# Gate columns of two convolution feed-forward layers: both activation parts in one 512-column product, added after PSUM

## The chip, the cores and the metric

One Trainium2 chip, one of its cores. The metric is the device time of one execution of the whole program in microseconds, as the median of several runs; a profile of one further execution gives the durations. The engines are called TensorE (PE in the profile; its weight loads are PEld), VectorE (DVE), ScalarE (ACT), GpSimd (POOL) and SyncE (SP), which here only starts transfers.

## The reference

Two transformer blocks over 256 tokens of width 1024, in float32. The change is in one function, which the second block calls once in each of its two layers:

```python
def conv_ffn(h, w_up, conv_w, conv_b, w_down):
    S = h.shape[1]
    u = h @ w_up                                        # 256 x 1024 @ 1024 x 5632
    up = jnp.pad(u, ((0, 0), (CONV_WIDTH_2 - 1, 0), (0, 0)))
    c = conv_b
    for i in range(CONV_WIDTH_2):                       # three taps along the tokens
        c = c + up[:, i:i + S] * conv_w[i]
    gate, val = c[..., :D_FF_2], c[..., D_FF_2:]        # 2816 each
    return (jax.nn.silu(gate) * val) @ w_down
```

The first block has a feed-forward layer without the convolution (`_swiglu`, "ffn0" in the kernel), which the change leaves as it is. The two with the convolution are "ffn1" and "ffn2". ffn2 is the last thing before the final norm.

## The kernel before

**Split products.** Nearly all products are done in three float32r matmuls. A weight tile W is split into w_hi, W rounded to float32r, and w_lo = W - w_hi; the activations likewise into a_hi and a_lo (inputs of a stage) or b_hi and b_lo (inputs of the second product of a stage). Each product is w_hi·a_hi + w_hi·a_lo + w_lo·a_hi, summed in PSUM (`three`, L468). A matmul loads a 128x128 weight block and streams 256 columns (the tokens) through it.

**Weights.** They come in slots of 8 blocks of 128x128 (512 KB) into a ring of six raw buffers (`w_raw`). For each slot ScalarE makes w_hi (L1187), and then VectorE makes w_lo (L1756), or for some slots GpSimd (L2602; `lo_on_pool` says which). w_hi and w_lo have rings of three, so the split of slot n may start only when TensorE is done with slot n-3. A slot gives TensorE 24 matmuls.

**A convolution feed-forward layer** (`ffn` in each engine's program). The 2816 hidden channels are 22 tiles of 128, f = 0 to 21. Per tile f there are three slots, in TensorE's order: the gate columns (g = 0), the value columns (g = 1), each 8 blocks over the 1024 inputs into one accumulator (PSUM banks 0 and 1 in turn), and the down product of an earlier tile (usually f-1), whose 8 outputs are kept in banks 4 to 7. In the two convolution layers GpSimd makes w_lo of the gate slots of f = 3 to 21, VectorE all others.

All engines' programs are written out in a fixed order, and an engine does its instructions in that order. For a tile f in the middle of the layer VectorE does:

1. g = 0: wait for the gate product; multiply the accumulator by the norm's factor into an SBUF tile (L2338, the eviction; it frees the accumulator); wait for ScalarE's first convolution tap (L1631); add the second tap (L2345) and the third (L2347);
2. g = 1: the same four for the value product;
3. wait for ScalarE's silu (L1640); multiply gate by value (L2359);
4. w_lo of the next tile's value slot (L1756), b_lo of the activation (L2371, after ScalarE's b_hi, L1650), w_lo of this tile's down slot (L1756); then the next tile.

ScalarE, for the same tile: the first tap of g = 0 (L1631), w_hi of the next tile's gate slot (L1187), the first tap of g = 1, silu, w_hi of the next value slot, b_hi, w_hi of the down slot. GpSimd waits for w_hi of the next tile's gate slot and makes its w_lo.

What ties them: TensorE can start a slot when its w_hi and w_lo are there, and an accumulator's next product when the eviction of the one before in that bank is done.

```python
x = FS[:, 2 * (f % 3) + g, :]
t = (name, 2 * f + g)
v.tensor_tensor(x, acc(t)[:, 0:T], R[:], ALU.mult).then_inc(
    *inc("ffn_scaled", ("fs", tag, f, g), ("acc", t)))
```

Of the kernel before, what the change touches and what calls it, by code (L numbers as in the profile page):

```python
# [17 lines left out]
P = 128  # L18
T = 256
D = 1024  # L20
KD = D // P
# [173 lines left out]
class Signals:  # L195
# [16 lines left out]
    def inc(self, label, *events, by=1):  # L212
        sem = self.sem(label)
        self.counts[label] += by
        for e in events:
            assert e not in self.events, e
            self.events[e] = (label, self.counts[label])
        return sem, by
# [48 lines left out]
def build(nc, io, known):  # L267
    with ExitStack() as ctx:
# [3 lines left out]
        def sb(name, shape, dt=F32):  # L272
            return ctx.enter_context(nc.sbuf_tensor(name, shape, dt))
# [3 lines left out]
                "p (a b) -> p a b", a=KD) for i in range(2))  # L277
        WHI = sb("w_hi", [P, SPLIT_SLOTS, 1024], F32R)
        WLO = sb("w_lo", [P, SPLIT_SLOTS, 1024], F32R)
        AH, AL = sb("a_hi", [P, KD, T], F32R), sb("a_lo", [P, KD, T], F32R)  # L280
        BH, BL = sb("b_hi", [P, KD, T], F32R), sb("b_lo", [P, KD, T], F32R)
        RAW = sb("w_raw", [P, RAW_SLOTS, 1024])
        H = sb("h", [P, KD, T])
# [43 lines left out]
        def acc(key):  # L327

            return bank[ACC_BANK[key]]
# [119 lines left out]
        def _(pe):  # L449
# [14 lines left out]
            def three(out, w, x, start, stop, weights_move=False, check=False):  # L464

                for n, (wi, xi) in enumerate(((0, 0), (0, 1), (1, 0))):
                    l, r = (x[xi], w[wi]) if weights_move else (w[wi], x[xi])
                    ins = mm(out, l, r, start=start and n == 0, stop=stop and n == 2, skip_group_check=check)  # L468
                return ins

            def blocks(s, b, n=1):
                c = slice(b * P, (b + n) * P)
                return WHI[:, ring(s), c], WLO[:, ring(s), c]

            def pair(x, k, cols=slice(0, T)):
                return x[0][:, k, cols], x[1][:, k, cols]
# [430 lines left out]
            def ffn(name, tag):  # L907

                s = FIRST[name]
                for f in range(NF + 1):  # L910
                    if f < NF:
                        for g in range(2):
                            out = acc_take((name, 2 * f + g))[:, 0:T]
                            slot_ready(s)
                            for k in range(KD):
                                if f == 0 and g == 0:
                                    pe.wait_ge(*at(("a_lo", tag, k)))
                                ins = three(out, blocks(s, k), pair(A, k), k == 0, k == KD - 1)
                            ins.then_inc(*inc("product_done", ("slot", s), (name, f, g)))
                            s += 1  # L920
                            if f == 0 and g == 0:
                                if tag in SUMMED:
                                    whole_mean_square(tag)
                                else:
                                    mean_square(tag, KD - 2)
                                    mean_square(tag, KD - 1)
                    for d in down_after(f):
                        slot_ready(s)
                        pe.wait_ge(*at(("act_lo", tag, d)))
                        for m in range(KD):  # L930
                            ins = three(bank[4 + m // 2][:, m % 2 * T:m % 2 * T + T], blocks(s, m),
                                        pair(B, d % 3), d == 0 and m % 2 == 0, f == NF, check=True)
                            if f == NF and m % 2 and m < KD - 1:
                                ins.then_inc(*inc("product_done", (name, "bank", m // 2)))
                        ins.then_inc(*inc("product_done", ("slot", s), (name, "down", d),
                                                      *([(name, "bank", 3)] if f == NF else [])))
                        s += 1
# [808 lines left out]
        def _(dve):  # L1746
# [14 lines left out]
            def step(ins, *events, label="vector_step"):  # L1761

                ins.then_inc(*inc(label, *events))
                dve.wait_ge(*last(label))
# [559 lines left out]
            def ffn(name, tag, tag_next, g_next, conv=None):  # L2324
                s = FIRST[name]
                ahead(s + 1)
                dve.wait_ge(*at(("r", tag)))
                for f in range(NF + 1):
                    if f < NF:
                        for g in range(2):  # L2330
                            ahead(s)
                            s += 1
                            dve.wait_ge(*at((name, f, g)))
                            if f >= 3 and conv is None:
                                dve.wait_ge(*at(("fa", tag, f - 3)))
                            x = FS[:, 2 * (f % 3) + g, :]
                            t = (name, 2 * f + g)
                            v.tensor_tensor(x, acc(t)[:, 0:T], R[:], ALU.mult).then_inc(  # L2338
                                *inc("ffn_scaled", ("fs", tag, f, g), ("acc", t)))
                            if f == 0 and g == 1:  # L2340
                                ahead(FIRST[name] + 2)
                            if conv is not None:
                                c = FC[:, 2 * (f % 2) + g, :]
                                dve.wait_ge(*at(("fc", tag, f, g)))
                                step(v.scalar_tensor_tensor(c[:, 1:T], x[:, 0:T - 1], par(f"cw{conv}", 44 + g * NF + f),  # L2345
                                                            c[:, 1:T], ALU.mult, ALU.add), label="ffn_conv")
                                v.scalar_tensor_tensor(c[:, 2:T], x[:, 0:T - 2], par(f"cw{conv}", g * NF + f),  # L2347
                                                       c[:, 2:T], ALU.mult, ALU.add).then_inc(
                                    *inc("ffn_conv", ("fcv", tag, f, g)))
                        dve.wait_ge(*at(("silu", tag, f)))  # L2350
                        if conv is not None:
                            dve.wait_ge(*at(("fcv", tag, f, 1)))
                        else:
                            dve.wait_ge(*at(("fs", tag, f, 1)))
                        if f >= 2:
                            dve.wait_ge(*at(("act_lo", tag, f - 2)))
                        src = (FS[:, 2 * (f % 3), :], FS[:, 2 * (f % 3) + 1, :]) if conv is None else \
                            (FC[:, 2 * (f % 2), :], FC[:, 2 * (f % 2) + 1, :])
                        v.tensor_tensor(FA[:, f % 2, :], src[0], src[1], ALU.mult).then_inc(  # L2359
                            *inc("ffn_act", ("fa", tag, f)))  # L2360
                    for n, _ in enumerate(down_after(f)):
                        if n == 0 or f == NF:
                            ahead(s + n)
                    s += len(down_after(f))
                    if name == "ffn0" and f == 9:
                        final_weights()
                    if name == "ffn0" and f == 11:
                        rope_args()
                    if f < NF:
                        dve.wait_ge(*at(("act_hi", tag, f)))  # L2370
                        v.tensor_tensor(BL[:, f % 3, :], FA[:, f % 2, :], BH[:, f % 3, :].bitcast(F32),  # L2371
                                        ALU.subtract).then_inc(*inc("ffn_act_lo", ("act_lo", tag, f)))
                    if f == NF - 1:
                        ahead(s - 1)
                for m in range(KD):
                    if m % 2 == 0:
                        dve.wait_ge(*at((name, "bank", m // 2)))
                    step(v.tensor_tensor(H[:, m, :], H[:, m, :], bank[4 + m // 2][:, m % 2 * T:m % 2 * T + T], ALU.add),
                         ("h", tag_next, m), label="h_made")
                    if g_next and m:  # L2380
                        lo_gained(tag_next, m - 1, A, H[:, m - 1, :], g_next)
                    if tag_next in NEXT_V and m in (4, 6):
                        ahead(SLOT[NEXT_V[tag_next], (m - 4) // 2])
                if g_next:
                    lo_gained(tag_next, KD - 1, A, H[:, KD - 1, :], g_next)
                if tag_next in NEXT_V:
                    ahead(SLOT[NEXT_V[tag_next], 2])
# [427 lines left out]
```

## Time and profile before

| | |
|---|---|
| time of three runs, median (lowest to highest) | 1211.64 us (1208.93 to 1212.19) |
| the profiled execution, its own time | 1210.1 us |
| its span | 1208.3 us |
| granted TensorE clock, mean | 0.995 of full speed |
| busy: TensorE / VectorE / ScalarE / GpSimd | 98% / 68% / 54% / 18% of the span |
| chain that ended last: TensorE / VectorE / ScalarE | 84% / 9% / 4% |

The page of the profile gives busy time by engine and by group of instructions; the lists in order of time ("timeline") give the start of each instruction, its duration and, in brackets, how long its engine sat idle before it and what ended that. The duration of a matmul is from its start to its modelled end, and matmuls overlap: the pace is read from the distance of their starts.

### The profile page before, as it was taken

To read this page: it belongs to the slowest core of one execution; us is meant where nothing else is said; L and a number is where in the kernel's file an instruction comes from. 1 tells how busy PE (TensorE), PEld (TensorE's weight loads), DVE (VectorE), ACT (ScalarE), POOL (GpSimd) and SP (SyncE) were. 2 spreads that over 40 slices of the span, in tenths; PEclk is the share of its full clock that TensorE was granted. 3 is DMA by queue.
4 is the path that set the end of the run, shared out by engine and by line. 5 is a ranking of instruction groups with operands and counts; after the bars stand their busy time and mean duration, and the time that the engine had idled before them with its cause. 6 is when DMAs were issued, how large, how long until landed. Compare 5 with 4: busy or idle time off the path is not lost.

```text
span 1208.3 us, 24091 instructions
## 1 busy us (share of the span) xinstructions
PE 1180.0 (98%) x9816; PEld 1111.9 (92%) x9816; DVE 819.6 (68%) x1472; ACT 656.3 (54%) x1128; POOL 214.6 (18%) x124
## 2 busy tenths in 40 slices
PE   9999999999999999999999999999999999999997
PEld 8888789999999999898898999999898878999997
DVE  6997856745544544678775776767655667777776
ACT  4347446645544444564566555555655566555554
POOL 2120000201122222021100223231121100322220
PEclk9999999999999999999999999999999989999999
DMA  8433334525656565543344566665433433665651
GB/s 342 139 108 115 112 124 141 168 94 181 199 179 188 178 188 177 162 137 100 114 140 145 170 187 180 188 179 171 160 124 121 140 123 109 187 189 179 189 178 36
DMA packets 51661, 188.60 MB, mean 156 GB/s; under 512 B 5728, under 2 KB 5856, under 8 KB 51040
## 3 DMA queue, kind: packets, MB, share of 16 engines
q1 hardware_dynamic: 51552, 187.07, 49.1%
q8 instruction: 78, 1.28, 0.4%
q14 instruction: 31, 0.25, 0.1%
HBM read 186.00 MB, written 1.05 MB: 155 GB/s over the span
## 4 chain that ended last, share of the span: by engine, by line
PE 84%; DVE 9%; ACT 4%; issue 2%; DMA 0%; POOL 0%; DVEq 0%; ACTq 0%
PE banks L468 65%; PE banks L498 7%; DVE w_lo L1756 2%; ACT w_hi L1187 2%; PE banks L541 1%; PE banks L972 1%; PE banks L526 1%; PE banks L986 1%; PE banks L589 1%; PE banks L952 1%; ACT arena L1631 1%; PE banks L889 1%; PE banks L866 1%; DVE arena L2345 1%; DVE arena L2347 0%
## 5 line engine op out<-in xcount | busy, mean ns | idle before, releaser
L1187 ACT ACTIVATE w_hi<-w_raw 128x1024 fp32r<-128x1024 f32 x313 | 328.9, 1052 | 179.4 <-PE banks L468 179.2
L468 PE MATMUL banks<-a_hi,w_hi 128*128 128x256 f32 x1432 | 410.7, 287 | 2.1 <-DVE w_lo L1756 1.1
L468 PE MATMUL banks<-a_lo,w_hi 128*128 128x256 f32 x1432 | 405.1, 283 | 0.0
L468 PE MATMUL banks<-a_hi,w_lo 128*128 128x256 f32 x1432 | 405.0, 283 | 0.0
L2602 POOL TENSOR_TENSOR w_lo<-w_raw,w_hi 128x1024 fp32r<-128x1024 f32 x80 | 194.8, 2435 | 844.5 <-ACT w_hi L1187 844.5
L1756 DVE TENSOR_TENSOR w_lo<-w_raw,w_hi 128x1024 fp32r<-128x1024 f32 x233 | 290.3, 1247 | 65.8 <-ACT w_hi L1187 64.6
L468 PEld LDWEIGHTS banks<-a_hi,w_hi 128*128 128x128 f32 x1432 | 274.5, 192 | 5.2 <-issue 3.5
L468 PEld LDWEIGHTS banks<-a_lo,w_hi 128*128 128x128 f32 x1432 | 274.6, 192 | 0.4
L468 PEld LDWEIGHTS banks<-a_hi,w_lo 128*128 128x128 f32 x1432 | 274.6, 192 | 0.0
L468 PE MATMUL banks<-b_hi,w_hi 128*128 128x256 f32 x880 | 253.6, 288 | 7.6 <-DVE h L2201 2.4
L468 PE MATMUL banks<-b_lo,w_hi 128*128 128x256 f32 x880 | 248.9, 283 | 0.0
L468 PE MATMUL banks<-b_hi,w_lo 128*128 128x256 f32 x880 | 248.8, 283 | 0.0
L468 PEld LDWEIGHTS banks<-b_hi,w_hi 128*128 128x128 f32 x880 | 168.6, 192 | 12.5 <-issue 4.1
L468 PEld LDWEIGHTS banks<-b_lo,w_hi 128*128 128x128 f32 x880 | 168.7, 192 | 0.3
L468 PEld LDWEIGHTS banks<-b_hi,w_lo 128*128 128x128 f32 x880 | 168.6, 192 | 0.0
L1631 ACT ACTIVATE arena<-arena,pars 128x256 f32<-128x256 f32 x88 | 53.0, 602 | 129.1 <-DVE arena L2338 129.1
L2338 DVE TENSOR_TENSOR arena<-banks,rstd 128x256 f32<-128x256 f32 x132 | 55.7, 423 | 86.9 <-PE banks L468 86.7
L2345 DVE SCALAR_TENSOR_TENSOR arena<-arena,pars 128x255 f32<-128x255 f32 x88 | 58.4, 664 | 57.7 <-ACT arena L1631 57.7
L498 PE MATMUL banks<-early,w_raw 128*128 128x256 f32 x368 | 82.0, 381 | 0.4 <-DVE early L1796 0.4
L498 PEld LDWEIGHTS banks<-early,w_raw 128*128 128x128 f32 x368 | 69.2, 190 | 10.6 <-DMA w_raw<-in_weights 0.6
L1650 ACT ACTIVATE b_hi<-arena 128x256 fp32r<-128x256 f32 x66 | 27.5, 417 | 39.1 <-DVE arena L2359 39.1
L1213 ACT ACTIVATE a_hi<-h,pars 128x256 fp32r<-128x256 f32 x64 | 32.2, 503 | 24.8 <-DVE h L2201 16.9
(396 smaller groups left out, 1311.3 us busy)
## 6 DMA issues: line engine op xcount, KB each, us to landing
w_raw<-in_weights SPq DMA_DIRECT2D x342, 512.0 KB, 3.6
arena<-in_mem SPq DMA_DIRECT2D x2, 1024.0 KB, 9.7
h<-in_x SPq DMA_DIRECT2D x1, 1024.0 KB, 5.3
early<-in_mem SPq DMA_DIRECT2D x1, 1024.0 KB, 15.5
out_h<-h SPq DMA_DIRECT2D x4, 256.0 KB, 2.6
cons<-in_cons SPq DMA_DIRECT2D x1, 546.0 KB, 7.8
arena<-in_late SPq DMA_DIRECT2D x1, 448.0 KB, 4.2
pars<-in_pars SPq DMA_DIRECT2D x1, 290.5 KB, 2.8
```

What stands on the lines that cost most here:

```text
L468: ins = mm(out, l, r, start=start and n == 0, stop=stop and n == 2, skip_group_check=check)
L498: ins = mm(out, raw(s, b % 8), x[:, k, :], start=n == 0, stop=n == K - 1)
L526: ins = mm(out, x[:, k, cols], raw(s, b * w % 8, w), start=k == 0, stop=k == K - 1)
L541: ins = mm(bank[2][:, 0:T] if out is None else out, ONES_D[:] if by is None else by, squares, start=m == 0, stop=m == KD - 1)
L1187: do(WHI[:, ring(n), :], RAW[:, n % RAW_SLOTS, :], ACT.Copy).then_inc(*inc("w_hi_made", ("w_hi", n)))
L1213: do(x[0][:, m, :], src, ACT.Copy, scale=par(g, m)).then_inc(*inc("input_hi", ("a_hi", tag, m)))
L1631: do(FC[:, 2 * (f % 2) + g, :], FS[:, 2 * (f % 3) + g, :], ACT.Identity, scale=par(f"cw{conv}", 88 + g * NF + f), bias=par(f"cb{conv}", g ...
L1650: do(BH[:, f % 3, :], FA[:, f % 2, :], ACT.Copy).then_inc(*inc("ffn_act_hi", ("act_hi", tag, f)))
L1756: v.tensor_tensor(WLO[:, ring(n), :], RAW[:, n % RAW_SLOTS, :], WHI[:, ring(n), :].bitcast(F32), ALU.subtract).then_inc(*inc("w_lo_made", ...
L2338: v.tensor_tensor(x, acc(t)[:, 0:T], R[:], ALU.mult).then_inc(*inc("ffn_scaled", ("fs", tag, f, g), ("acc", t)))
L2345: step(v.scalar_tensor_tensor(c[:, 1:T], x[:, 0:T - 1], par(f"cw{conv}", 44 + g * NF + f), c[:, 1:T], ALU.mult, ALU.add), label="ffn_conv")
L2602: g.tensor_tensor(WLO[:, ring(n), :], RAW[:, n % RAW_SLOTS, :], WHI[:, ring(n), :].bitcast(F32), ALU.subtract).then_inc(*inc("w_lo_pool", ...
```

## The change

- The split activations a_hi and a_lo of a stage are now two halves of one buffer, `a_parts`, so that for each of the 8 input blocks they lie side by side.
- In ffn1 and ffn2, for the gate slots alone (g = 0), w_hi is loaded once per block and streams a_hi and a_lo as one matmul of 512 columns: w_hi·a_hi goes to the left half of the accumulator's bank, w_hi·a_lo to the right half. w_lo·a_hi (256 columns) is added into the left half. 16 matmuls per gate slot instead of 24, with as many columns.
- VectorE then adds the two halves from PSUM with a tensor_reduce over pairs that lie 256 elements apart (the accumulator is free after it), and after a wait for its own result multiplies the SBUF tile by the norm's factor in place. The value slots keep their one multiplication.

```diff
-        AH, AL = sb("a_hi", [P, KD, T], F32R), sb("a_lo", [P, KD, T], F32R)
+        A_PARTS = sb("a_parts", [P, KD, 2, T], F32R)
+        AH, AL = (A_PARTS[:, :, i, :] for i in range(2))
...
-                                ins = three(out, blocks(s, k), pair(A, k), k == 0, k == KD - 1)
+                                if name != "ffn0" and g == 0:
+                                    w = blocks(s, k)
+                                    mm(acc((name, 2 * f + g)), w[0], A_PARTS[:, k, :, :].rearrange("p a b -> p (a b)"),
+                                       start=k == 0, stop=False)
+                                    ins = mm(out, w[1], AH[:, k, :], start=False, stop=k == KD - 1)
+                                else:
+                                    ins = three(out, blocks(s, k), pair(A, k), k == 0, k == KD - 1)
...
-                            v.tensor_tensor(x, acc(t)[:, 0:T], R[:], ALU.mult).then_inc(
-                                *inc("ffn_scaled", ("fs", tag, f, g), ("acc", t)))
+                            if conv is not None and g == 0:
+                                step(v.tensor_reduce(x, acc(t).rearrange("p (h t) -> p t h", h=2), AX.X, ALU.add), ("acc", t),
+                                     label="ffn_halves")
+                                v.tensor_tensor(x, x, R[:], ALU.mult).then_inc(*inc("ffn_scaled", ("fs", tag, f, g)))
+                            else:
+                                v.tensor_tensor(x, acc(t)[:, 0:T], R[:], ALU.mult).then_inc(
+                                    *inc("ffn_scaled", ("fs", tag, f, g), ("acc", t)))
```

VectorE's order in the middle of ffn1, one tile before the change (the tile's step 1 to step 4, then the next tile's first eviction):

```order
777 L2338 TENSOR_TENSOR arena<-banks,rstd 128x256
778 L2345 SCALAR_TENSOR_TENSOR arena<-arena,pars 128x255
779 L2347 SCALAR_TENSOR_TENSOR arena<-arena,pars 128x254
780 L2338 TENSOR_TENSOR arena<-banks,rstd 128x256
781 L2345 SCALAR_TENSOR_TENSOR arena<-arena,pars 128x255
782 L2347 SCALAR_TENSOR_TENSOR arena<-arena,pars 128x254
783 L2359 TENSOR_TENSOR arena<-arena 128x256
784 L1756 TENSOR_TENSOR w_lo<-w_raw,w_hi 128x1024
785 L2371 TENSOR_TENSOR b_lo<-arena,b_hi 128x256
786 L1756 TENSOR_TENSOR w_lo<-w_raw,w_hi 128x1024
787 L2338 TENSOR_TENSOR arena<-banks,rstd 128x256
```

The same place after the change (line numbers are 7 to 12 higher):

```order
787 L2346 TENSOR_REDUCE arena<-banks 128x256
788 L2348 TENSOR_TENSOR arena<-arena,rstd 128x256
789 L2357 SCALAR_TENSOR_TENSOR arena<-arena,pars 128x255
790 L2359 SCALAR_TENSOR_TENSOR arena<-arena,pars 128x254
791 L2350 TENSOR_TENSOR arena<-banks,rstd 128x256
792 L2357 SCALAR_TENSOR_TENSOR arena<-arena,pars 128x255
793 L2359 SCALAR_TENSOR_TENSOR arena<-arena,pars 128x254
794 L2371 TENSOR_TENSOR arena<-arena 128x256
795 L1763 TENSOR_TENSOR w_lo<-w_raw,w_hi 128x1024
796 L2383 TENSOR_TENSOR b_lo<-arena,b_hi 128x256
797 L1763 TENSOR_TENSOR w_lo<-w_raw,w_hi 128x1024
798 L2346 TENSOR_REDUCE arena<-banks 128x256
```

One instruction more per tile, a reduce in front of the multiplication; nothing else changes place.

## Rows read from the trace of the kernel before

**Rows 1.** The page, part 1: busy us, share of the span, instructions.

```profile
PE 1180.0 (98%) x9816; PEld 1111.9 (92%) x9816; DVE 819.6 (68%) x1472; ACT 656.3 (54%) x1128; POOL 214.6 (18%) x124
```

**Rows 2.** The chain that ended last, in order of time: start us, us, what.

```profile
670.52 1.14 DVE w_lo L1756
671.80 158.80 PE banks L468 x1320
...
841.92 1.13 DVE w_lo L1756
...
1023.31 158.81 PE banks L468 x1320
```

**Rows 3.** Timeline, VectorE early in ffn1: start us, duration, instruction [idle before, what ended it].

```profile
664.73 0.41 DVE L2338 TENSOR_TENSOR arena<-banks,rstd 128x256 f32<-128x256 f32 x1
...
673.10 0.42 DVE L2338 TENSOR_TENSOR arena<-banks,rstd 128x256 f32<-128x256 f32 x1
674.18 0.48 DVE L2345 SCALAR_TENSOR_TENSOR arena<-arena,pars 128x255 f32<-128x255 f32 x1 [0.67 <-ACT arena L1631]
674.70 0.48 DVE L2347 SCALAR_TENSOR_TENSOR arena<-arena,pars 128x254 f32<-128x254 f32 x1
675.10 0.42 DVE L2338 TENSOR_TENSOR arena<-banks,rstd 128x256 f32<-128x256 f32 x1
676.20 1.67 DVE L2345 SCALAR_TENSOR_TENSOR arena<-arena,pars 128x255 f32<-128x255 f32 x1 [0.67 <-ACT arena L1631]
...
678.47 0.43 DVE L2359 TENSOR_TENSOR arena<-arena 128x256 f32<-128x256 f32 x1
...
679.95 0.42 DVE L2371 TENSOR_TENSOR b_lo<-arena,b_hi 128x256 fp32r<-128x256 f32 x1
680.33 1.23 DVE L1756 TENSOR_TENSOR w_lo<-w_raw,w_hi 128x1024 fp32r<-128x1024 f32 x1
681.48 0.41 DVE L2338 TENSOR_TENSOR arena<-banks,rstd 128x256 f32<-128x256 f32 x1
```

**Rows 4.** Timeline, ScalarE and GpSimd in the same stretch.

```profile
673.55 0.60 ACT L1631 ACTIVATE arena<-arena,pars 128x256 f32<-128x256 f32 x1 [1.63 <-DVE arena L2338]
674.06 1.04 ACT L1187 ACTIVATE w_hi<-w_raw 128x1024 fp32r<-128x1024 f32 x1
...
675.18 2.40 POOL L2602 TENSOR_TENSOR w_lo<-w_raw,w_hi 128x1024 fp32r<-128x1024 f32 x1 [64.77 <-ACT w_hi L1187]
```

**Rows 5.** Timeline, VectorE in the middle and at the end of ffn1.

```profile
741.35 0.42 DVE L2338 TENSOR_TENSOR arena<-banks,rstd 128x256 f32<-128x256 f32 x1 [0.16 <-PE banks L468]
...
745.32 0.80 DVE L2345 SCALAR_TENSOR_TENSOR arena<-arena,pars 128x255 f32<-128x255 f32 x1 [0.67 <-ACT arena L1631]
...
749.99 0.42 DVE L2338 TENSOR_TENSOR arena<-banks,rstd 128x256 f32<-128x256 f32 x1 [0.17 <-PE banks L468]
...
827.75 0.42 DVE L2338 TENSOR_TENSOR arena<-banks,rstd 128x256 f32<-128x256 f32 x1 [0.16 <-PE banks L468]
...
836.13 0.42 DVE L2338 TENSOR_TENSOR arena<-banks,rstd 128x256 f32<-128x256 f32 x1
```

**Rows 6.** Two lines' own view: count, duration ns min/median/max, first and last start us.

```profile
L2338 DVE TENSOR_TENSOR arena<-banks,rstd x132: 414/424/425, 309.3 to 1190.8; 128x256 f32<-128x256 f32 x132
L2345 DVE SCALAR_TENSOR_TENSOR arena<-arena,pars x88: 477/485/1670, 658.9 to 1191.9; 128x255 f32<-128x255 f32 x88
```

**Rows 7.** Groups of VectorE instructions: busy us, mean ns of one, idle before.

```profile
L2359 DVE TENSOR_TENSOR arena<-arena 128x256 f32<-128x256 f32 x66 | 29.5, 447 | 6.0
...
L2228 DVE TENSOR_REDUCE small<-banks 128x2 f32<-128x512 f32 x12 | 7.9, 687 | 5.4 <-PE banks L866 5.3
...
L2260 DVE TENSOR_REDUCE small<-banks 128x2 f32<-128x256 f32 x12 | 5.1, 422 | 12.3 <-PE banks L979 12.3
```

**Rows 8.** Timeline, TensorE: 512-column matmuls, nine starts apart.

```profile
120.16 0.39 PE L468 MATMUL banks<-w_lo,b_hi 128*128 128x512 f32 x1
...
122.20 0.40 PE L468 MATMUL banks<-w_lo,b_hi 128*128 128x512 f32 x1
```

## The prediction

> **What bounds the kernel now.** The busy shares come first: TensorE 98%, VectorE 68% [rows 1]. By this TensorE is the bound and VectorE has a third of its time to spare, so that a change that takes matmuls from TensorE and gives VectorE 0.7 us per tile looks harmless. The chain by time says the same of the inside of the two layers: 1320 matmuls follow one another over 158.80 us in ffn1 and 158.81 us in ffn2, with VectorE's w_lo on the chain before and after such a stretch [rows 2]. That is 0.1203 us per 256-column matmul, 8.64 to 8.66 us for a tile's 72.
>
> But a share does not tell how long a loop of waits is. So I follow one tile on VectorE early in ffn1, where it lags behind TensorE: neither gate eviction there has idle time before it, so its own work sets its pace. The first evictions of three tiles stand at 664.73, 673.10 and 681.48 us [rows 3]: 8.38 us from the second to the third. Let s be the gate eviction, 673.10. ScalarE's first tap starts 0.45 later and w_hi of the next gate slot at s + 0.96; GpSimd starts its w_lo at s + 2.08 and ends it at 677.58, s + 4.48 [rows 4]. VectorE comes to the second tap of the value half (L2345) at 676.20, and this instruction, which takes 0.48 elsewhere, takes 1.67: it ends at 677.87, 0.29 after GpSimd [rows 3]. Both of its tensors lie in SBUF. The eviction L2338, which reads PSUM, never takes over 0.425, though it too runs beside GpSimd (675.10, from 0.08 before GpSimd starts); L2345 goes from 0.477 to 1.670 [rows 3, 6]. In the middle of the layer it takes 0.80 [rows 5]. I read this as a hold: the tap waits for GpSimd to finish. From there VectorE has no real pause: the gate-by-value product at 678.47, w_lo, b_lo, w_lo, and the next gate eviction at 681.48 [rows 3].
>
> So there is a **loop that TensorE is not part of**: gate eviction, ScalarE's tap, w_hi, GpSimd's w_lo, VectorE's held tap, two w_lo, next gate eviction, 8.38 us. TensorE's tile takes 8.64. The loop's slack is 0.26 us, and where TensorE sets the pace VectorE idles just 0.16 to 0.17 us before the gate eviction [rows 5]. VectorE's other idle time (0.67 before each L2345) is inside the loop and no reserve.
>
> **The change, part by part.**
>
> *TensorE.* Per gate slot 16 matmuls of 256 become 8 of 512. Nine starts of 512-column matmuls span 2.04 us [rows 8], 0.227 each, against 2 x 0.1203 = 0.241. Gain 0.014 x 8 = 0.11 us per tile: TensorE's tile becomes 8.53. Over 44 tiles that is 4.9 us if TensorE were the bound. These rows stream weights through activations, but are the same instruction and width.
>
> The Trainium skill, "TensorE: Matmul & The Clock Gate", section "Back-to-back issue gap", gives about 131 ns for a sustained 512-column matmul; that would save 0.11 us per matmul, 0.88 per tile. No run here comes near it: 0.227 stands in the trace. It would not change my sum either, since TensorE is not the bound after the change.
>
> *VectorE.* Out: a 0.42 us eviction. In: a reduce over 512 PSUM elements, a wait on its own result, and an SBUF multiplication. The reduce of 128x512 from PSUM takes 0.687, that of 128x256 0.422 [rows 7]; both read side by side elements and write two. The new one reads its pairs 256 elements apart and writes 256. Bounds: 0.42, if writing half as many elements as it reads sets the pace, and 1.22, if every element costs double (0.422 - 0.265 = 0.157 fixed, 512 x 2.07 ns on top, twice the 265/256 of these rows). I take 0.69, the row with the same input. The wait: L2345 to its dependent L2347, 674.66 to 674.70, so 0.03 to 0.04 [rows 3]. The multiplication: 0.43, as L2359 unheld (678.47) [rows 3]. Together 1.14 for 0.42: **+0.72 us per tile**, 0.45 to 1.25 by the bounds.
>
> *Where it lies.* All of it is at the head of the loop: the first tap waits for the multiplication, w_hi is behind the tap on ScalarE, GpSimd behind w_hi, the held tap behind GpSimd, and both w_lo, b_lo and the next eviction are queued behind that tap. The loop becomes 8.38 + 0.72 = 9.10 us, above TensorE's 8.53. TensorE then waits before each gate slot for GpSimd's w_lo, some 0.57 us per tile. The value eviction isn't delayed beyond the shift, and the accumulator is free after 0.69 instead of 0.42, while its bank is wanted again some 5.7 us later: nothing. The new multiplication has two SBUF operands and could be held too, but runs at s + 0.72 to s + 1.14, and GpSimd at s + 2.80 to s + 5.20: no meeting. SyncE's transfers wait for w_lo of six slots before, two tiles of time: nothing. The joined buffer a_parts moves no instruction.
>
> *Sum per layer.* From f = 2 to f = 20 there are 18 intervals, 154.65 us now (673.10 to 827.75) [rows 3, 5]; at 9.10 they are 163.80: +9.15. The other four gate evictions (f = 0, 1, the last interval, and f = 21 itself) lie where VectorE is late already, with intervals of 8.37 and 8.38 and VectorE's w_lo on the chain [rows 2, 3, 5]: 4 x 0.72 = 2.88. Together 12.0 us. This is 22 x 0.72 = 15.8 less the 3.8 of slack that the 18 intervals hold over 8.38. ffn2 has the same stretch to 0.01 us [rows 2], and the kernel's end follows it. Twice: 24.1. The profiled execution's 1210.1 us becomes 1234.2; the median of the runs shown is 1.5 above it, and I give 1235.
>
> **The rivals.**
>
> *A, the strided reduce is slow.* Every second element read lies 1 KB away. With the bound of 1.22 the addition is 1.25 per tile: 22 x 1.25 - 3.8 = 23.7 per layer, +47, 1258. Halfway (a reduce of 0.95) it is 22 x 0.98 - 3.8 = 17.8, +36, 1247. No row of before reads in such an order; the reduce rows speak only for the element count.
>
> The Trainium skill, "Vector Engine (DVE) Microarchitecture Reference", section 5.2, has a table by which a port that hops at each element loses some 0.65 cycle per element, yet notes that a one-source read that alternates between two regions ran at the full rate. The table would make the reduce some 0.35 us longer, an estimate from that page, and the time about 1250; the note leaves 1235. Both are of SBUF, and no run here shows it for PSUM.
>
> *B, the reduce is cheap,* 0.42 us: +0.45 per tile, 22 x 0.45 - 3.8 = 6.1 per layer, 1222. Against it: 265 ns more for 256 more inputs [rows 7].
>
> *C, no hold in the loop (not slower).* If L2345 is long for another reason than GpSimd's end, one that doesn't move with the gate eviction, the loop is 1.19 shorter in the rest: 7.19 + 0.72 = 7.91, below TensorE's 8.53. Then the 18 intervals gain 0.11 each and only the ends of the layers lose: 2 x (4 x 0.72 - 2.0) = +1.8, 1212 to 1213, no change. It decides at an addition that leaves the loop under 8.53; with the hold that is 0.15 us, which even B exceeds. Against it: the tap's end follows GpSimd's by 0.29 in the row where it takes 1.67.
>
> *D, the 512-column matmul is not one pass* at full pace, and TensorE loses. It would have to lose 0.57 us per tile before it counted; at 0.227 [rows 8] nothing speaks for it.
>
> **Numbers.** My forecast (reduce 0.65 to 0.8) has 0.72, centre 1235, by itself 1230 to 1241. A has 0.12, B and in-between values 0.08, C 0.06, D 0.02. The range, 1222 to 1250, takes in B and most of A. A measurement of this kernel can tell about 0.3% (3.6 us) from no change: slower 0.94 (forecast, A, B, D), same 0.05 (C), faster 0.01 (C with a cheap reduce).
>
> **What would show it.** Gate reduces 9.1 us apart from f = 2 on, without idle time before them; the value half's second tap at about 1.67 us for 19 tiles of each layer; TensorE idle about half a microsecond before each gate slot, released by GpSimd's w_lo; TensorE's 1320 matmuls no longer one piece. Wrong if the distance is 8.5 (C), or if the reduce row is not near 0.69 (A, B).

## The result and the profile after

The changed kernel takes 1234.28 us (1233.31 to 1235.5, four runs) against 1210.29 us of the kernel before in the same session (1208.81 to 1212.19): ratio 1.0197, 95% interval 1.0178 to 1.0215. It is **slower by 24.0 us** (21.5 to 26.0 by that interval), where 24.1 was forecast.

Three lines of the page of the changed kernel: the span, the busy time (part 1), and the chain that ended last, by engine (part 4).

```profile
span 1233.7 us, 23431 instructions
...
PE 1187.1 (96%) x9464; PEld 1095.7 (89%) x9464; DVE 873.9 (71%) x1516; ACT 656.6 (53%) x1128; POOL 214.7 (17%) x124
...
PE 57%; DVE 32%; ACT 8%; issue 3%; DMA 0%; POOL 0%; DVEq 0%; ACTq 0%
```

Against [rows 1], the shares hardly move: VectorE from 68 to 71%, TensorE from 98 to 96%. The chain tells much more: TensorE's part was 84% and is 57, VectorE's was 9% and is 32. The loop has become the bound, and yet GpSimd, which is a member of it, has 0% of the chain. Why, the timeline shows. One tile in the middle of ffn1, VectorE (start us, duration, instruction, [idle before, what ended it]); it answers to [rows 3] and [rows 5]:

```profile
739.54 0.68 DVE L2346 TENSOR_REDUCE arena<-banks 128x256 f32<-128x512 f32 x1
740.25 0.42 DVE L2348 TENSOR_TENSOR arena<-arena,rstd 128x256 f32<-128x256 f32 x1
741.35 0.48 DVE L2357 SCALAR_TENSOR_TENSOR arena<-arena,pars 128x255 f32<-128x255 f32 x1 [0.67 <-ACT arena L1638]
741.87 0.48 DVE L2359 SCALAR_TENSOR_TENSOR arena<-arena,pars 128x254 f32<-128x254 f32 x1
742.27 0.42 DVE L2350 TENSOR_TENSOR arena<-banks,rstd 128x256 f32<-128x256 f32 x1
743.36 1.68 DVE L2357 SCALAR_TENSOR_TENSOR arena<-arena,pars 128x255 f32<-128x255 f32 x1 [0.67 <-ACT arena L1638]
...
747.51 1.23 DVE L1763 TENSOR_TENSOR w_lo<-w_raw,w_hi 128x1024 fp32r<-128x1024 f32 x1
748.66 0.68 DVE L2346 TENSOR_REDUCE arena<-banks 128x256 f32<-128x512 f32 x1
```

and GpSimd and TensorE in the same tile:

```profile
742.34 2.42 POOL L2614 TENSOR_TENSOR w_lo<-w_raw,w_hi 128x1024 fp32r<-128x1024 f32 x1 [6.70 <-ACT w_hi L1194]
```

```profile
744.33 0.28 PE L469 MATMUL banks<-b_hi,w_lo 128*128 128x256 f32 x1
744.90 0.47 PE L921 MATMUL banks<-a_parts,w_hi 128*128 128x512 f32 x1 [0.29 <-POOL w_lo L2614]
745.21 0.28 PE L923 MATMUL banks<-a_parts,w_lo 128*128 128x256 f32 x1
```

The reduces stand 9.12 us apart here and 9.09 to 9.12 in all intervals of both layers but the first, without idle time before them. GpSimd's w_lo ends at 744.76, the tap of the value half at 745.04, 0.28 later, where the row early in ffn1 of before gave 0.29 [rows 3, 4]. The hold is inside the instruction's duration, and no semaphore stands for it. So neither the chain nor the list of waits can put it down to GpSimd. It looks like a slow tap. What gives it away is the spread of one line (L2357: 479 to 1684 ns) and the other engine's end.

TensorE stops once a tile: from 744.33 to 744.90, 0.57 us between starts where 0.12 is the pace. It is released by GpSimd. So it loses 0.45 us there, where the prediction had 0.57. Two of VectorE's lines by themselves (count, duration ns min/median/max):

```profile
L2346 DVE TENSOR_REDUCE arena<-banks x44: 682/684/689, 659.1 to 1212.4; 128x256 f32<-128x512 f32 x44
...
L2348 DVE TENSOR_TENSOR arena<-arena,rstd x44: 424/426/428, 659.8 to 1213.1; 128x256 f32<-128x256 f32 x44
```

From the first gate eviction of ffn1 to the last, the changed kernel takes 189.75 us (659.05 to 848.80) against 178.36 (657.77 to 836.13): +11.4. In ffn2 it is 189.78 against 178.36, the same.

The profiled spans differ by 25.4 us, a little more than the medians. Of these, 1.3 are there before ffn1 begins: its first gate eviction is at 659.05 instead of 657.77. They arise between 130 and 150 us, where the instructions are the same but the joined buffer `a_parts` is already in place. From 142 to 146 us the granted clock is 0.67 where it was 1.00 before, and starts of 512-column matmuls stand 0.43 apart (141.78 to 142.21) instead of 0.23, the pace of the lower of the clock's two levels. At 298 us, before the first changed product of any kernel here, the six profiled kernels that have `a_parts` (the changed one and five of the experiments) are 1.2 to 3.3 us behind the kernel before; the other four are within 0.6 us of it. From 130 to 146 us the granted clock is 0.71 to 0.80 in the six and 0.89 in each of the five others. So this piece goes with the joined buffer. Why is not shown.

### The profile page after: what moved, and what is told of

Its sections match the earlier page's. It is cut to its first block, busy times and chain, and to the rows that moved or that the text cites. A ratio compares the mean times of both kernels' runs of the same rounds, so it can differ in the third digit from the quotient of the medians.

```text
span 1233.7 us, 23431 instructions
## 1 busy us (share of the span) xinstructions
PE 1187.1 (96%) x9464; PEld 1095.7 (89%) x9464; DVE 873.9 (71%) x1516; ACT 656.6 (53%) x1128; POOL 214.7 (17%) x124
## 4 chain that ended last, share of the span: by engine, by line
PE 57%; DVE 32%; ACT 8%; issue 3%; DMA 0%; POOL 0%; DVEq 0%; ACTq 0%
PE banks L469 38%; DVE w_lo L1763 9%; DVE arena L2357 7%; PE banks L499 7%; ACT arena L1638 4%; DVE arena L2359 3%; DVE arena L2346 2%; ACT w_hi L1194 2%; DVE arena L2348 2%; DVE arena L2371 2%; DVE arena L2350 1%; DVE b_lo L2383 1%; PE banks L542 1%; PE banks L979 1%; PE banks L527 1%
## 5 line engine op out<-in xcount | busy, mean ns | idle before, releaser
L469 PE MATMUL banks<-a_parts,w_hi 128*128 128x256 f32 x2160 | 397.8, 285 | 2.6 <-DVE w_lo L1763 1.2
L469 PEld LDWEIGHTS banks<-a_parts,w_hi 128*128 128x128 f32 x2160 | 336.6, 191 | 8.1 <-issue 4.6
L469 PE MATMUL banks<-a_parts,w_lo 128*128 128x256 f32 x1080 | 305.3, 283 | 0.0
L469 PEld LDWEIGHTS banks<-a_parts,w_lo 128*128 128x128 f32 x1080 | 206.6, 191 | 0.0
L921 PE MATMUL banks<-a_parts,w_hi 128*128 128x512 f32 x352 | 129.0, 406 | 13.2 <-POOL w_lo L2614 11.6
L2357 DVE SCALAR_TENSOR_TENSOR arena<-arena,pars 128x255 f32<-128x255 f32 x88 | 87.5, 995 | 57.7 <-ACT arena L1638 57.7
L923 PE MATMUL banks<-a_parts,w_lo 128*128 128x256 f32 x352 | 98.8, 281 | 0.0
L921 PEld LDWEIGHTS banks<-a_parts,w_hi 128*128 128x128 f32 x352 | 66.0, 188 | 33.9 <-issue 19.9
L2350 DVE TENSOR_TENSOR arena<-banks,rstd 128x256 f32<-128x256 f32 x88 | 37.0, 421 | 55.8 <-PE banks L469 55.8
L923 PEld LDWEIGHTS banks<-a_parts,w_lo 128*128 128x128 f32 x352 | 66.5, 189 | 0.1
```

Source lines behind the costliest of these rows:

```text
L921: mm(acc((name, 2 * f + g)), w[0], A_PARTS[:, k, :, :].rearrange("p a b -> p (a b)"), start=k == 0, stop=False)
L923: ins = mm(out, w[1], AH[:, k, :], start=False, stop=k == KD - 1)
```

## The experiments

Nine kernels, each timed in turn with the kernel before. Ratios are to it. Line numbers are each kernel's own.

**VectorE's part alone.** In the kernel before:

```diff
+if conv is not None and g == 0:
+    step(v.tensor_reduce(x, acc(t)[:, 0:T].unsqueeze(2).to_broadcast([P, T, 2]), AX.X, ALU.max),
+         ("acc", t), label="ffn_halves")
+    v.tensor_tensor(x, x, R[:], ALU.mult).then_inc(*inc("ffn_scaled", ("fs", tag, f, g)))
+else:
     v.tensor_tensor(x, acc(t)[:, 0:T], R[:], ALU.mult).then_inc(...)
```

> The kernel before with VectorE's part of the change alone: the gate eviction is a reduce over 512 PSUM elements (each of the 256 sums read twice, maximum of the pair, so the values stay), the wait, and the multiplication in SBUF; TensorE keeps its 24 matmuls of 256 columns per gate slot. Theory (a loop of eviction, tap, w_hi, GpSimd's w_lo, held tap, two w_lo goes from 8.38 to 9.10 us per tile and passes TensorE's 8.64): gate reduces 9.1 us apart, 1234 us, the same as the changed kernel within 1 us, since TensorE's saving is behind the loop. Rival 1 (the 512-column product or its bank is what costs): about 1210. Rival 2 (TensorE's saving of 0.11 us per tile counts even now): 1239.

Measured: 1234.11 us, ratio 1.0202 (1.0187 to 1.0218). VectorE's reduces in the middle of ffn1:

```profile
746.78 0.68 DVE L2339 TENSOR_REDUCE arena<-banks 128x256 f32<-128x512 f32 x1
...
755.88 0.68 DVE L2339 TENSOR_REDUCE arena<-banks 128x256 f32<-128x512 f32 x1
```

9.10 apart. With TensorE's half of the change taken away the time is the same to 0.2 us: the loss is that of VectorE's addition, within the noise of some 2 us, and none of TensorE's saving arrives. This reduce reads each element twice in a row, and takes 683 ns in the median, where the changed kernel's, with its pairs 256 elements apart, takes 684.

**TensorE's part alone.** In the changed kernel the eviction is the old one for all tiles, so that the right half of the accumulator, w_hi·a_lo, is left out of the result:

```diff
-if conv is not None and g == 0:
+if False:
     step(v.tensor_reduce(...))
```

> The changed kernel with the old eviction: the 512-column product stays, but VectorE evicts the left half alone with one multiplication, so the w_hi x a_lo term of the gate columns of the two layers is left out of the result. Theory: the loop is 8.38 again and TensorE, now 8.53 per tile, is the bound; some 20 tiles of a layer gain 0.11 each, 2.2 us per layer, 1206 us. Rival 1 (the 512-column product costs time): above 1210. Rival 2 (the saving is hidden): 1210.

Measured: 1207.71 us, ratio 0.9983 (0.9974 to 0.9992), a gain of 2.2 us where 4 was expected. TensorE, in a gate slot:

```profile
749.95 0.40 PE L921 MATMUL banks<-a_parts,w_hi 128*128 128x512 f32 x1
750.19 0.28 PE L923 MATMUL banks<-a_parts,w_lo 128*128 128x256 f32 x1
750.30 0.40 PE L921 MATMUL banks<-a_parts,w_hi 128*128 128x512 f32 x1
750.53 0.28 PE L923 MATMUL banks<-a_parts,w_lo 128*128 128x256 f32 x1
750.65 0.40 PE L921 MATMUL banks<-a_parts,w_hi 128*128 128x512 f32 x1
```

A pair takes 0.35 us, against 3 x 0.1203 = 0.361. Gate evictions stand 8.59 apart where they stood 8.64: the saving is 0.05 us per tile, half of the 0.11 I had taken from a run of 512-column matmuls alone. In turn with 256-column ones the wide matmul takes 0.23 to 0.24. From the first gate eviction to the last a layer takes 177.40 us instead of 178.36, so the most that the change could have brought here is some 2 us, 0.2%.

**The GpSimd work started earlier.** On ScalarE, in the changed kernel:

```diff
                             s += 1
+                            if conv is not None and g == 0 and f:
+                                ahead(s)
                             if conv is not None:
                                 act.wait_ge(*at(("fs", tag, f, g)))
```

> The changed kernel with one thing moved on ScalarE: w_hi of the next tile's gate slot stands ahead of the first tap of the gate half, not behind it. It waits for TensorE alone, so GpSimd's w_lo no longer starts behind VectorE's reduce and multiplication. VectorE has the same instructions in the same order. Theory: GpSimd ends before the value half's second tap, whose row goes from 1.67 to 0.48 us; the loop falls from 9.10 to 7.9, TensorE is the bound again; the head and tail of each layer keep some 2 us, TensorE gains 2.2: 1210 us, plus or minus 3. Rival (VectorE has simply more work than fits into a tile): 1234.

Measured: 1245.12 us, ratio 1.0296 (1.0281 to 1.0312). The expectation was wrong by 35 us. VectorE, then GpSimd:

```profile
743.63 0.68 DVE L2348 TENSOR_REDUCE arena<-banks 128x256 f32<-128x512 f32 x1
744.35 1.91 DVE L2350 TENSOR_TENSOR arena<-arena,rstd 128x256 f32<-128x256 f32 x1
...
748.94 0.48 DVE L2359 SCALAR_TENSOR_TENSOR arena<-arena,pars 128x255 f32<-128x255 f32 x1 [0.67 <-ACT arena L1640]
...
753.03 0.68 DVE L2348 TENSOR_REDUCE arena<-banks 128x256 f32<-128x512 f32 x1
```

```profile
743.49 2.49 POOL L2616 TENSOR_TENSOR w_lo<-w_raw,w_hi 128x1024 fp32r<-128x1024 f32 x1 [6.91 <-ACT w_hi L1194]
```

The tap of the value half is free, as expected: 0.48. But GpSimd now runs from 743.49 to 745.98, over the new multiplication, which has both operands in SBUF: 1.91 us for 0.42, ending 0.28 after GpSimd. The interval is 9.40. The hold costs 1.49 in place of 1.19, and so the loop is 0.3 longer and not 1.19 shorter. The prediction had checked that the two don't meet at the given times; the experiment moved one of them and I did not check again. Nor does the early w_hi wait for TensorE alone, as expected: on ScalarE it stands behind b_hi and w_hi of the down slot, and so behind VectorE's gate-by-value product (750.03; b_hi at 750.49; both w_hi from 750.81 to 752.80; GpSimd at 752.88). It is again a loop that TensorE is not part of. The run shows the hold more sharply than the planned outcome would have: it goes with the two operands and the overlap, not with the line.

**GpSimd out of the two layers.** `lo_on_pool` returns False for them:

```diff
+    if name in ("ffn1", "ffn2"):
+        return False
     if name[:3] == "ffn":
```

> The changed kernel with GpSimd out of the two layers: VectorE makes w_lo of their gate slots too. Theory: no tap is held any more (0.48 us each), but VectorE has 1.22 us more per tile in the same loop, where the hold cost 1.19; the interval of f = 1, where GpSimd has no part now either, is 9.1 already, so all of them are 9.1 and the time is 1234, plus or minus 2. Rival (the hold is what costs, and nothing else): 1210 to 1215. Rival (VectorE's busy time decides): over 1245.

Measured: 1232.81 us, ratio 1.0188 (1.0171 to 1.0205). The tap's line, as above:

```profile
L2359 DVE SCALAR_TENSOR_TENSOR arena<-arena,pars x88: 479/483/488, 660.9 to 1214.3; 128x255 f32<-128x255 f32 x88
```

No tap is held (the maximum is 0.488), the reduces are 9.07 to 9.10 apart, and the time is as good as with GpSimd's help. GpSimd takes 1.22 us of work per tile from VectorE and gives it back as a hold of 1.19: in this loop its help was worth nothing.

**Earlier start, and the sum in PSUM.** The third experiment's edit, and:

```diff
-step(v.tensor_reduce(x, acc(t).rearrange("p (h t) -> p t h", h=2), AX.X, ALU.add), ("acc", t),
+step(v.tensor_reduce(bank[3][:, 0:T], acc(t).rearrange("p (h t) -> p t h", h=2), AX.X, ALU.add),
      label="ffn_halves")
-v.tensor_tensor(x, x, R[:], ALU.mult).then_inc(*inc("ffn_scaled", ("fs", tag, f, g)))
+v.tensor_tensor(x, bank[3][:, 0:T], R[:], ALU.mult).then_inc(
+    *inc("ffn_scaled", ("fs", tag, f, g), ("acc", t)))
```

> The changed kernel with the early w_hi of the third experiment, and the sum of the halves written to PSUM (a free bank) instead of SBUF, so that the multiplication behind it reads one operand from SBUF and not two. Theory (GpSimd's w_lo holds whichever VectorE instruction with two SBUF operands meets it; in the third experiment that was the new multiplication, 1.91 us for 0.42): the multiplication takes 0.42 beside GpSimd, both second taps together are held 0.3 to 0.9, the loop is about 8.2 us, and TensorE at 8.59 per tile is the bound again: gate reduces 8.6 us apart, 1213 us, plus or minus 3. Rival (the early w_hi itself costs, by its place on ScalarE): reduces still 9.4 apart, 1245. Rival (too much work on VectorE): 1234.

Measured: 1213.48 us, ratio 1.0032 (1.0022 to 1.0043).

```profile
752.99 0.69 DVE L2348 TENSOR_REDUCE banks<-banks 128x256 f32<-128x512 f32 x1
753.72 0.43 DVE L2350 TENSOR_TENSOR arena<-banks,rstd 128x256 f32<-128x256 f32 x1
754.82 1.13 DVE L2360 SCALAR_TENSOR_TENSOR arena<-arena,pars 128x255 f32<-128x255 f32 x1 [0.67 <-ACT arena L1640]
...
757.47 0.48 DVE L2360 SCALAR_TENSOR_TENSOR arena<-arena,pars 128x255 f32<-128x255 f32 x1 [0.67 <-ACT arena L1640]
```

```profile
753.27 2.40 POOL L2617 TENSOR_TENSOR w_lo<-w_raw,w_hi 128x1024 fp32r<-128x1024 f32 x1 [6.18 <-ACT w_hi L1194]
```

The same reduce and the same multiplication, now with one operand in PSUM, run beside GpSimd in 0.69 and 0.43 us. The gate tap is held for 0.65, and the reduces stand 8.60 apart (744.39 to 752.99), TensorE's pace. VectorE has every instruction of the changed kernel, and of the 24 us only 3.4 are left (each against the kernel before in its own session). So it was not the amount of work. What remains is for the most part the ends of the layers, where VectorE is late anyway: from the first reduce to the last it is 179.78 us, 1.4 more than before, and the first two intervals have grown by 0.7 each. The two edits were made together; the sum in PSUM without the early start was not run.

**Two doses.** In the kernel before, ahead of each gate eviction of the two layers, with 16 or 256 for N:

```diff
+if conv is not None and g == 0:
+    step(v.tensor_scalar(x[:, 0:N], acc(t)[:, 0:N], 1.0, None, ALU.mult), label="ffn_halves")
 v.tensor_tensor(x, acc(t)[:, 0:T], R[:], ALU.mult).then_inc(...)
```

> The kernel before, with one small instruction ahead of each gate eviction of the two layers: VectorE multiplies 16 PSUM columns by one into the eviction's target, and the eviction waits for it. About 0.2 us more per tile. Theory: the loop goes to 8.58, still under TensorE's 8.64; only the four gate evictions per layer at its ends show it: 4 x 0.2 x 2 = 1.6 us, 1211.5. Rival (every addition on VectorE counts in full): 44 x 0.2 = 8.8, 1219.

> As the small dose, but with 256 columns, so 0.45 us more per tile. Theory: the loop goes to 8.83, past 8.64; per layer 22 x 0.45 less the 3.8 of slack = 6.1, together 12.2, 1222. Rival (VectorE is busy 68%, the work fits beside TensorE's): 1210 to 1212. Rival (in full): 1230.

The inserted lines, small and large:

```profile
L2339 DVE TENSOR_SCALAR arena<-banks x44: 165/168/177, 657.5 to 1186.9; 128x16 f32<-128x16 f32 x44
```

```profile
L2339 DVE TENSOR_SCALAR arena<-banks x44: 416/418/419, 657.3 to 1198.1; 128x256 f32<-128x256 f32 x44
```

The small dose adds 0.20 us with its wait, 8.8 us of VectorE in all, and costs 0.7 us: 1210.72, ratio 1.0014 (1.0004 to 1.0025), so 0.5 to 3.0 us; 1.6 was expected. In the trace the 18 intervals in the middle of a layer grow by 0.2 us together, of 3.6 added, and the two at the start and the one at the end by 0.2 each. The large adds 0.45, 19.8 us in all, and costs 12: 1222.30, ratio 1.0110 (1.0092 to 1.0128), with evictions 8.84 apart (8.83 expected). With the changed kernel's 0.72 and 24 us these three points fit one line with a corner: next to nothing in the middle of a layer up to 0.26 us per tile, and in full beyond.

**The same change where VectorE waits.** The joined product and the sum in ffn0 alone, for both its slots, and the old eviction in ffn1 and ffn2. The diff is against the changed kernel:

```diff
-if name != "ffn0" and g == 0:
+if name == "ffn0":
...
-if conv is not None and g == 0:
+if conv is None:
-    step(v.tensor_reduce(x, acc(t).rearrange("p (h t) -> p t h", h=2), AX.X, ALU.add), ("acc", t),
+    step(v.tensor_reduce(bank[3][:, g * T:(g + 1) * T], acc(t).rearrange("p (h t) -> p t h", h=2), AX.X, ALU.add),
+         ("acc", t),
...
-    v.tensor_tensor(x, x, R[:], ALU.mult).then_inc(...)
+    v.tensor_tensor(x, bank[3][:, g * T:(g + 1) * T], R[:], ALU.mult).then_inc(...)
```

> The kernel before with the joined 512-column product and VectorE's sum in the other feed-forward layer, ffn0, for gate and up columns, and nowhere else (sum to PSUM, then the multiplication). There VectorE idles 2.5 us before the second eviction of a tile, waiting for TensorE. Theory: the 0.72 us more per eviction are covered in the middle of the layer; TensorE gains 0.05 per slot as the second experiment showed, 44 slots: -2.2 us, and the first and last tiles give back up to 1.5: 1208 to 1210, a gain of at most 0.2%. Rival (the addition costs as in the other layers): above 1225.

Measured: 1206.74 us (twelve runs), ratio 0.9977 (0.9965 to 0.9988): **faster than both kernels**, by 0.2%, and a little more than the 1208 to 1210 expected. VectorE in a tile of ffn0:

```profile
393.93 0.70 DVE L2346 TENSOR_REDUCE banks<-banks 128x256 f32<-128x512 f32 x1 [1.66 <-PE banks L923]
394.67 0.42 DVE L2348 TENSOR_TENSOR arena<-banks,rstd 128x256 f32<-128x256 f32 x1
...
399.63 0.70 DVE L2346 TENSOR_REDUCE banks<-banks 128x256 f32<-128x512 f32 x1 [0.44 <-PE banks L923]
```

The stretch of ffn0 from TensorE's restart to the next layer's first product, in the kernel before and in this one (us, busy of PE, PEld, DVE, ACT, POOL):

```profile
309.82:495.55 185.73, 184.57 (x1536) 184.40 (x1537) 95.77 (x147) 84.93 (x116) 45.62 (x19) 1.00 0.59 183
```

```profile
311.34:494.62 183.28, 182.12 (x1201) 166.37 (x1201) 122.65 (x191) 87.98 (x116) 45.58 (x19) 1.00 0.58 185
```

VectorE does 27 us more work in a stretch that becomes 2.45 us shorter, where 44 slots of 0.05 make 2.2. Of the 44 reduces 37 have idle time before them, ended by TensorE; the seven without are those of the first two tiles, one in the middle, and the two of the last. In ffn1 the first evictions of [rows 3] had none. The other stretches explain why the whole came out lower than expected: the 1.5 us of `a_parts` are lost ahead of ffn0, and 2.4 us are gained between 950 and 1010 us, where nothing was changed and the granted clock is 1.00 against 0.94 in the profile of before. Two other profiled kernels, the one without GpSimd and the small dose, gain the same 2.4 us there, and change nothing in ffn0. So it is not to be counted for this change, and what it comes from is not shown.

**The early start in the kernel before.** The third experiment's edit alone:

> The kernel before with nothing but the early w_hi of the third experiment on ScalarE: w_hi of the next gate slot ahead of the first tap of the gate half. The gate eviction here has one SBUF operand and can't be held. Theory: VectorE's loop without a hold is 7.2 us and with one self-adjusting, so TensorE's 8.64 is the pace from the first tile on in place of 8.38 while VectorE lags, but TensorE itself isn't faster: 1210 to 1212, no gain; what it costs at the ends of a layer is what the fifth experiment has beyond 2 x 4 x 0.72 less 2.2. Rival (the early w_hi frees the loop and with it time): below 1208.

Measured: 1211.07 us, ratio 1.0009 (0.9999 to 1.0019). Evictions are 8.64 apart from the fifth interval on, TensorE's pace. The gate tap:

```profile
751.86 1.93 DVE L2347 SCALAR_TENSOR_TENSOR arena<-arena,pars 128x255 f32<-128x255 f32 x1 [0.67 <-ACT arena L1633]
```

It is held for 1.45 us; without that the interval would be 7.19. An earlier start for GpSimd brings nothing where TensorE is the bound. No gate eviction has idle time before it any more: the hold has taken up all the slack, and an eviction without idle time is not by itself a sign that VectorE sets the pace.

## Why the prediction was right

- **The bound.** The step that decided was to measure the loop where TensorE doesn't set the pace: 8.38 us in the first tiles. The doses show it as a threshold: 0.20 us hidden, 0.45 not. One reading beside it was incomplete. Where TensorE sets the pace, VectorE idles before the gate eviction for 0.16 to 0.17 us, and before the value eviction too:

```profile
744.23 0.42 DVE L2338 TENSOR_TENSOR arena<-banks,rstd 128x256 f32<-128x256 f32 x1 [0.78 <-PE banks L468]
```

That 0.78 is no reserve: the tap behind it is held for 0.32 there instead of 1.19 [rows 5], and ends with GpSimd either way. The slack is the difference of the intervals, 0.26, and not the sum of the idle times.
- **The hold by GpSimd.** Read from one line's spread and one coincidence of ends, it is shown by the runs: the tap is 0.48 without GpSimd, the multiplication is held when GpSimd is moved over it, and is not held when its input lies in PSUM; the ends keep 0.28. The kernel before shows it over its whole length: all 38 second taps that start inside a w_lo of GpSimd end 0.27 to 0.29 us after it, and none of the 55 evictions L2338 that start inside one takes over 0.425. With the hold cut to 0.65 and off the new multiplication, 20.6 of the 24 us are back. Rival C falls. The prediction had it right that the new multiplication doesn't meet GpSimd.
- **The addition,** 0.72 us: reduce 0.684 (0.69 taken), multiplication 0.426 (0.43), wait 0.03. The row with the same number of inputs was the right one; rivals A and B fall. Reading pairs 1 KB apart from PSUM costs nothing here: 684 ns against 683 for the same element read twice. Of the two statements of the Trainium skill's "Vector Engine (DVE) Microarchitecture Reference", section 5.2, both of SBUF, the note on the alternating one-source read agrees with what PSUM shows here, 684 ns; the table's loss per hop does not appear.
- **The sum.** Intervals of 9.09 to 9.12 for 9.10; from first to last gate reduce +11.4 for 11.3; 24.0 for 24.1 us. The first two are as good as the forecast looks. That the medians agree to 0.1 us is luck: their interval is 21.5 to 26.0, and the profiled spans differ by 25.4, with the 1.3 us ahead of ffn1.
- **A term at nothing.** The prediction says that the joined buffer moves no instruction. It adds and reorders none, but in every profiled kernel that has it 1.2 to 3.3 us are lost ahead of ffn0. No row of the kernel before shows it, and its cause stays open.
- **One term was mis-sized: TensorE's saving,** 0.11 us per tile, measured 0.05. The row was of 512-column matmuls in a row, and not of ones in turn with 256-column ones; that the alternation makes the difference is likely, but no run separates it from the operands, which differ too. It stood behind the loop, so the sum did not feel it. A forecast for a kernel bound by TensorE would have been too hopeful by half, as the second experiment's was. Rival D (TensorE loses) falls too. The some 131 ns that the Trainium skill, "TensorE: Matmul & The Clock Gate", section "Back-to-back issue gap", gives for a sustained 512-column matmul are not reached in any run here: 0.227 us is the lowest pace.

## What to carry to other kernels

A third of idle time on an engine says nothing of how much can be added to it: find a stretch where it lags, with intervals shorter than the bound's and no idle time before the first instruction, and compare its interval there with the bound's. What is over (here 0.26 us per tile) is the reserve; the same two instructions, with the sum in PSUM, were free in ffn0, where nearly every eviction waits for TensorE. And when an instruction's row has a wide spread, look at what GpSimd is doing at its end: moving GpSimd's start passed the hold on to another instruction with two SBUF operands, and moving an operand of that one to PSUM took it off again; what was left of it fell on the tap.

## What was not expected of the hardware

- The hold went to the new multiplication (1.91 us for 0.42) as soon as GpSimd started 0.86 us before it.
- A 512-column matmul in turn with 256-column ones saves 0.05 us per eight blocks, 0.006 of a block's 0.361, where a run of them by themselves promised 0.014. And each wait of TensorE costs a little more than its length: in the changed kernel the first wide matmul after each of the 38 waits for GpSimd stands 0.30 to 0.31 before its successor (744.90 to 745.21), and 0.23 to 0.24 otherwise.
- The hold regulates itself: in the two early-start kernels that run at TensorE's pace the gate tap is stretched (1.13 us with the sum in PSUM, 1.93 in the kernel before) by just as much as keeps VectorE at that pace, since GpSimd's start hangs on TensorE (ScalarE's w_hi ahead of it idles 0.31 to 0.38 us for it) and the tap on VectorE.
- The held instruction's whole length seems to come behind GpSimd's end. One of 255 or 256 elements ends 0.27 to 0.29 us after it. The six w_lo of VectorE, 1024 elements, that start inside one of GpSimd's in the kernel before end 1.08 to 1.09 after it, here 604.31 after 603.23:

```profile
602.27 2.04 DVE L1756 TENSOR_TENSOR w_lo<-w_raw,w_hi 128x1024 fp32r<-128x1024 f32 x1 [0.81 <-ACT w_hi L1187]
```

```profile
600.83 2.40 POOL L2602 TENSOR_TENSOR w_lo<-w_raw,w_hi 128x1024 fp32r<-128x1024 f32 x1 [21.38 <-ACT w_hi L1187]
```
